# A two-block forward pass on one core: four places where the order of work is changed

## The reference

```
h = x * (1 + sc1) + sh1                          # six modulation rows from w_ada
z, xbc, dt, q, k, v, f = split(h @ w_in)
xs, B, C = split(silu(conv4(xbc)))               # Mamba-2 scan, 16 heads of 64, 4 chunks of 128
y_ssm = rms_norm((scan(xs, dt, A, B, C) + d_skip * xs) * silu(z))
y_att = rms_norm(forgetting_attention(q, k, v, log_sigmoid(f)))     # 16 heads, causal
x = layer_norm(ALPHA * x + (1 + g1) * (concat(y_ssm, y_att) @ w_out))
h = x * (1 + sc2) + sh2
x = layer_norm(ALPHA * x + (1 + g2) * (relu(h @ w_ff_in)**2 @ w_ff_out))
# second block
q, k, v, gb, gc, hin, u = split(rms_norm(x) @ w_in_2)
mix = concat(band_attention(norm(q), norm(k), v), gated_conv(gb, gc, hin), pooling(u))
x = x + mix @ w_out_2
x = x + relu(rms_norm(x) @ w_mlp1_2)**2 @ w_mlp2_2
```

## Time and profile before

| what | value |
|---|---|
| median of 3 runs | 1455.87 us (1450.27 to 1456.78) |
| the profiled execution | 1452.82 us |
| its span, first to last instruction | 1451.1 us |
| mean granted TensorE clock | 0.995 |
| busy share PE, DVE, ACT, POOL | 96%, 47%, 38%, 45% |

### The profile page before, as it was taken

How to read it: one execution, slowest core, us unless ns; L and a number is a source line. 1 busy time by engine, 2 the same in 40 slices (tenths; PEclk the granted TensorE clock), 3 DMA queues, 4 the chain that set the end, 5 groups by cost and what they waited for, 6 DMA issues and landing times.

```text
span 1451.1 us, 17537 instructions
## 1 busy us (share of the span) xinstructions
PE 1398.9 (96%) x6751; PEld 1163.2 (80%) x6751; DVE 679.5 (47%) x991; ACT 546.0 (38%) x792; POOL 659.1 (45%) x523
## 2 busy tenths in 40 slices
PE   2999999999999989999999998999999999999999
PEld 2887787888888878888888876877888888888887
DVE  6677968766622882141325456346514214132131
ACT  0635453576554163141332325324425214133231
POOL 0543855332233855445445544841144544544442
PEclk9999999999999999999999999999999999999999
DMA  9353346633214333232232232320022232223222
GB/s 332 109 146 89 88 146 185 194 118 115 88 31 145 120 90 112 92 107 91 87 116 87 87 116 77 99 87 30 30 88 87 87 103 100 87 88 114 87 92 82
DMA packets 126552, 153.29 MB, mean 106 GB/s; under 512 B 5564, under 2 KB 89808, under 8 KB 126496
## 3 DMA queue, kind: packets, MB, share of 16 engines
q1 hardware_dynamic: 123760, 146.95, 31.9%
q0 software_dynamic: 2192, 5.49, 1.1%
q10 hardware_dynamic: 544, 0.10, 0.0%
HBM read 150.32 MB, written 2.21 MB: 105 GB/s over the span
## 4 chain that ended last, share of the span: by engine, by line
PE 87%; DVE 6%; POOL 3%; ACT 2%; issue 1%; DMA 1%; SPq 0%; DVEq 0%; POOLq 0%; ACTq 0%
PE bank L1558 25%; PE bank L1560 25%; PE bank L1559 25%; PE bank L1703 3%; POOL w_lo L520 2%; PE bank L1693 2%; DVE tmp L1126 1%; PE bank L2050 1%; DMA arena<-in_w_ada_dram 1%; PE bank L1678 1%; PE bank L1874 1%; PE bank L1818 1%; PE bank L1875 1%; ACT w_hi L675 1%; PE bank L1668 1%
## 5 line engine op out<-in xcount | busy, mean ns | idle before, releaser
L520 POOL TENSOR_TENSOR w_lo<-raw,w_hi 128x512 fp32r<-128x512 f32 x428 | 585.6, 1399 | 679.6 <-ACT w_hi L675 678.5
L1558 PE MATMUL bank<-w_hi,a_hi 128*128 128x512 f32 x928 | 365.4, 394 | 13.0 <-DVE a_lo L1037 6.0
L1560 PE MATMUL bank<-w_hi,a_lo 128*128 128x512 f32 x928 | 362.6, 391 | 0.0
L1559 PE MATMUL bank<-w_lo,a_hi 128*128 128x512 f32 x928 | 362.4, 390 | 0.0
L675 ACT ACTIVATE w_hi<-raw 128x2048 fp32r<-128x2048 f32 x107 | 204.8, 1914 | 349.6 <-PE bank L1560 346.6
L1558 PE MATMUL bank<-a_hi,w_hi 128*128 128x512 f32 x800 | 315.6, 394 | 3.4 <-DVE a_lo L1037 2.5
L1560 PE MATMUL bank<-a_hi,w_lo 128*128 128x512 f32 x800 | 312.1, 390 | 0.0
L1559 PE MATMUL bank<-a_lo,w_hi 128*128 128x512 f32 x800 | 312.0, 390 | 0.0
L1558 PEld LDWEIGHTS bank<-w_hi,a_hi 128*128 128x128 f32 x928 | 175.1, 189 | 51.6 <-POOL w_lo L520 6.5
L1560 PEld LDWEIGHTS bank<-w_hi,a_lo 128*128 128x128 f32 x928 | 174.9, 189 | 37.1
L1559 PEld LDWEIGHTS bank<-w_lo,a_hi 128*128 128x128 f32 x928 | 175.2, 189 | 35.5
(11 more groups left out here) (231 smaller groups left out, 1190.1 us busy)
## 6 DMA issues: line engine op xcount, KB each, us to landing
raw<-in_w_mlp_dram SPq DMA_DIRECT2D x32, 1024.0 KB, 5.1
raw<-in_w_in_dram SPq DMA_DIRECT2D x24, 1024.0 KB, 5.2
arena<-in_w_ada_dram SPq DMA_DIRECT2D x18, 1024.0 KB, 5.4
raw<-in_w_ff_in_dram SPq DMA_DIRECT2D x16, 1024.0 KB, 5.3
raw<-in_w_ff_out_dram SPq DMA_DIRECT2D x16, 1024.0 KB, 5.0
raw<-in_w_out_dram SPq DMA_DIRECT2D x12, 1024.0 KB, 5.1
raw<-in_w_in_dram SPq DMA_DIRECT2D x16, 512.0 KB, 5.2
arena<-in_w_ada_dram SPq DMA_DIRECT2D x3, 2048.0 KB, 17.9
```

Source lines behind the costliest of these rows:

```text
L520: last = pool.tensor_tensor(w_lo[:, u0 % 2, cols], raw[:, u0 % 2, cols], w_hi[:, u0 % 2, cols].bitcast(F32), ALU.subtract)
L1558: pe.matmul(out_, hi_a, hi_b, start=start, stop=False)
L1559: pe.matmul(out_, hi_a, lo_b, start=False, stop=False)
L1560: return pe.matmul(out_, lo_a, hi_b, start=False, stop=stop)
```

## The change

The four places are changed like this.

1. `turn_xs(6)` and `turn_xs(7)` come ahead of `z_half(0, 0)` on TensorE. ScalarE's list is as it was.
2. TensorE does `v_half(2, 0)`, `v_half(3, 0)`, `v_half(2, 1)`, `v_half(3, 1)` in place of (2, 0), (2, 1), (3, 0), (3, 1). The tiles lie in banks 0 to 3 in place of 4, 5, 0, 1. ScalarE rounds unit U_QK1 at once after unit U_V + 3, and reads the tiles out later, around the first head's exponentials.
3. ScalarE reads two wo1 tiles ahead of the rounding of U_WO1 + 3. TensorE's second gate row (`g_row(40, ...)`) goes to banks 6 and 7 and ahead of `wo1_half(3, 0)`, and its copies ahead of the first four turned tiles.
4. The first unit of the second block's projection is done for token tiles 0 and 1 over all four k, and then for tiles 2 and 3. It starts when two low parts are made, not four.

```diff
--- before.py
+++ after.py
@@ -108,7 +108,7 @@
             ((6, 2, 8), (7, 0, 1)), ((7, 1, 8),), (), ())
 MIX_K = (6, 7, 4, 5)
 REL_BANKS = ((5, 6), (1, 2))
-V_BANKS = ((4, 5), (0, 1))
+V_BANKS = ((0, 1), (2, 3))
 N3_BANKS = (4, 5, 6, 7, 4, 5, 6, 7)
 
 WO1_HALF = {14: (0, 0), 15: (0, 1), 16: (1, 0), 17: (1, 1)}
@@ -887,14 +887,13 @@
             hi(U_V + 2)
             read_rows(U_V, 0, lambda t: vtok[:, t, 0:512])
             hi(U_V + 3)
+            hi(U_QK1)
 
             def read_v(d):
 
-                act.wait_ge(ticks, 2 * U_V + 2 * d + 2)
+                act.wait_ge(ticks, 2 * (U_V + 3) + d - 1)
                 for n in range(2):
                     act.activation(vtok[:, 2 * (d - 2) + n, 512:1024], bank[V_BANKS[d - 2][n]][:], ACT.Copy).then_inc(evac[1], 1)
-
-            read_v(2)
 
             def wo1_tile(n):
                 act.wait_ge(ticks, 2 * U_WO1 + 2 * (n // 2) + 2)
@@ -912,35 +911,35 @@
                 return bank[b][:, o:o + (q + 1) * P]
 
             for s in range(18):
-                if s == 2:
-                    read_v(3)
+                if s == 1:
+                    read_v(2)
                 elif 3 <= s < 15:
                     split_hi(s + 1, (s - 1) % 2)
                 elif s == 16:
                     wo1_tile(0)
                     wo1_tile(1)
-                if s == 1:
-                    hi(U_QK1, late=1)
-                elif s == 14:
+                if s == 14:
                     hi(U_WO1 + 1)
                 if s >= 2:
                     copy_probT(s - 2, probT)
                 if 1 <= s < 17:
                     probabilities(s - 1, score, prob)
+                if s == 1:
+                    read_v(3)
                 if s % 2 == 0 and 2 <= s < 14:
                     hi(U_QK1 + s // 2)
                 elif s == 17:
                     hi(U_WO1 + 2, late=1)
-            hi(U_WO1 + 3)
             wo1_tile(2)
             wo1_tile(3)
+            hi(U_WO1 + 3)
             wo1_tile(4)
             wo1_tile(5)
             g_row(0, 4, 0)
+            act.wait_ge(ext_out, 32)
+            g_row(1, 6, 3)
             for k in range(4):
                 turned_hi(R_ATT, 1, k, ATT_BANKS[k], v1[:, V_ATT + k:V_ATT + k + 1])
-            act.wait_ge(ext_out, 32)
-            g_row(1, 4, 3)
             act.wait_ge(ticks, 2 * U_WO1 + 7)
             hi(U_WO2)
             act.wait_ge(ticks, 2 * U_WO1 + 8)
@@ -1597,12 +1596,14 @@
                 for j in range(0 if t0 is None else 2, 4):
                     column_tile(u0 + j // 2, j % 2, act_buf, bank[4 * s + j][:], None, i, per)
 
-            def row_half(u0, b, s, act_buf, kk0, first, final, wait=None, i=0, per=0):
+            def row_half(u0, b, s, act_buf, kk0, first, final, wait=None, i=0, per=0, halves=False):
 
 
                 slot = (u0 + b) % 2
                 pe.wait_ge(w_lo_made, at(i, per, u0 + b + 1))
                 order = [(k, t) for k in range(4) for t in range(TB)] if b == 0 else [(k, t) for t in range(TB) for k in range(4)]
+                if halves:
+                    order = [(k, t) for pair in range(2) for k in range(4) for t in (2 * pair, 2 * pair + 1)]
                 for m, (k, t) in enumerate(order):
                     kk = kk0 + k
                     if wait and t == 0:
@@ -1616,13 +1617,13 @@
                     elif b == 1 and m % 8 == 3:
                         last.then_inc(even_done, 1)
 
-            def row_pair(u0, s, n_use, act_buf, t0=None, i=0, per=0, uses=0, tstep=0):
+            def row_pair(u0, s, n_use, act_buf, t0=None, i=0, per=0, uses=0, tstep=0, halves=False):
 
                 if n_use:
                     pe.wait_ge(evac[s], at(i, 4 * uses, 4 * n_use))
                 for b in range(2):
                     wait = None if t0 is None else lambda kk: at(i, tstep, t0 + kk + 1)
-                    row_half(u0, b, s, act_buf, 4 * b, b == 0, b == 1, wait, i, per)
+                    row_half(u0, b, s, act_buf, 4 * b, b == 0, b == 1, wait, i, per, halves and b == 0)
 
             def turn_blocks(turn, n0):
 
@@ -1837,9 +1838,11 @@
             turn_xs(4)
             turn_xs(5)
             pe.wait_ge(cb_evac, 2)
+            turn_xs(6)
+            turn_xs(7)
             z_half(0, 0)
-            for m in range(6, 10):
-                turn_xs(m)
+            turn_xs(8)
+            turn_xs(9)
             z_half(0, 1)
             pe.wait_ge(xs_made, 10)
             ssd_chunk(0)
@@ -1890,20 +1893,23 @@
             late_columns(0)
             row_half(U_V, 1, 0, 0, 4, False, True)
             late_columns(1)
+            pe.wait_ge(evac[0], 4 * N_V[0] + 2)
             v_half(2, 0)
             late_columns(2)
-            v_half(2, 1)
+            pe.wait_ge(evac[0], 4 * (N_V[0] + 1))
+            v_half(3, 0)
             late_columns(3)
-            pe.wait_ge(evac[0], 4 * (N_V[0] + 1))
 
             for s in range(18):
+                if s == 2:
+                    pe.wait_ge(evac[1], 4 * N_V[1] + 4)
                 if s >= 2:
                     probs_t(s - 2, prob)
                 if s < 2:
-                    v_half(3, s)
+                    v_half(2 + s, 1)
                 elif s < 14:
                     if s < 4:
-                        pe.wait_ge(evac[1], 4 * N_V[1] + s + 1)
+                        pe.wait_ge(evac[1], 4 * N_V[1] + s - 1)
                     else:
                         pe.wait_ge(qk_lo, 2 * s + 2)
                     column_tile(U_QK1 + s // 2 - 1, s % 2, 0, bank[s % 2][:])
@@ -1911,7 +1917,6 @@
                     wo1_half(*WO1_HALF[s])
                 if s == 0:
                     pe.wait_ge(ones_set, 4)
-                    pe.wait_ge(evac[1], 4 * N_V[1] + 2)
                 if s >= 2:
                     h = s - 2
                     values(h, probT, lambda k: vtok[:, k, h * HD:h * HD + HD])
@@ -1927,14 +1932,13 @@
             pe.wait_ge(late_made, 1)
             g_row(16, 4)
             wo1_half(2, 1)
+            pe.wait_ge(pt_made, 48)
+            g_row(40, 6)
             wo1_half(3, 0)
-            pe.wait_ge(pt_made, 48)
+            pe.wait_ge(g_made, 4)
             pe.wait_ge(o_made, 16)
             turn(att, 4, 0, ATT_BANKS)
-            pe.wait_ge(g_made, 2)
-            g_row(40, 4)
             wo1_half(3, 1)
-            pe.wait_ge(g_made, 4)
             pe.wait_ge(a_lo_made, T_ATT + 4)
             turn(att, 4, 4, ATT_BANKS)
             pe.wait_ge(yacc_read, 8)
@@ -1954,8 +1958,8 @@
 
             feed_forward(U_FF1, T_X1, T_HID1, N_FF1)
             turn_blocks(1, N_QKV2)
-            pe.wait_ge(a_lo_made, T_N2 + 4)
-            row_pair(U_QKV2, 0, N_QKV2[0], 0, T_N2)
+            pe.wait_ge(a_lo_made, T_N2 + 2)
+            row_pair(U_QKV2, 0, N_QKV2[0], 0, T_N2, halves=True)
             row_pair(U_QKV2 + 2, 1, N_QKV2[1], 0)
             row_pair(U_QKV2 + 4, 0, N_QKV2[0] + 1, 0)
```

## The result

The changed kernel took 1457.76 us (median of 10 executions, 1453.7 to 1460.46). The kernel before, beside it, took 1450.7 us (10 executions, 1450.27 to 1458.2). The ratio is 1.0032, with a 95% interval of 1.0016 to 1.0047. By the ratio, which goes over all executions, that is 4.6 us slower, within 0.5%, as forecast (sum +4.2 us, time 1458.5). Of all executions in this document two took 2875.7 and 7073.6 us, and they stand in no ratio. The profiled execution took 1458.13 us, its span was 1456.4 us and its mean granted clock 0.993.

A forecast was written before the change was run, and what follows sets the result against it. TensorE, busy for 96% of the span, was taken as the bound. Terms +1.5 + 1.7 - 1.8 + 1.7 - 1.5 + 0.9 + 1.7 = +4.2 us gave 1457.0 or 1460.1; forecast 1458.5, range 1451.5 to 1464.

The forecast's parts named there:

- Place 1 (+3.2): Transpositions ahead of the gate: TensorE waits for the twelfth activation, +1.5 us, with a clock fall of +1.7 us.
- Rival 4: All four places work as their order suggests, the first costing nothing: -8.3 us, 1444.5 to 1447.6 us; chance 0.04.
- Place 2 (-0.1): Value tiles by first halves: old wait and fall go, new 2.4 us wait for exponentials, net -1.8, fall +1.7 us.
- I take the fall, +1.7 us: Value tiles: the new 2.4 us wait, close to 2.52 us that cost a fall, is followed by one of 1.7 us.
- the -4.2: Value tiles, best bound: -4.2 us if DVE were free, from the value weight's wait (2.52 us) and its fall (1.7).
- Place 3 (-1.5): Last projection: earlier readings and gate row bring the output weight's products from 465.24 to 464.1; -1.5 us, bounds -0.8 and -1.7.
- Place 4 (+2.6): Second block's query rows: 2.6 us won first, then lost to longer DVE passes; fourth unit 0.9 us later, fall +1.7 us.
- can't start before 889.27: Second block's query rows: DVE's eight activation passes must wait until 889.27 us, when a row lands by DMA.
- Rival 1: DVE's passes aren't lengthened and the query rows win 1.4 us: total +0.2, 1453.0 to 1456.1 us; chance 0.17.
- Rival 2: The clock hardly falls, or falls at other moments: sum -0.9 without three falls, 1451.9 to 1455.0 us; chance 0.17.
- Rival 3: Query rows cascade: fourth weight's low part takes 8 us, TensorE stands 7; total +7.8, 1460.6 to 1463.7 us; chance 0.12.

The follow-up runs named there:

- place 4 alone: The kernel before with only the second block's query rows done by token pairs, starting when two low parts are made; ratio 0.9997 (0.9978 to 1.0015).
- place 3 and place 4 alone: Two runs of the kernel before: only the last projection reordered, ratio 1.0005; only the second block's query rows by token pairs, ratio 0.9997.

## Why the prediction was right, point by point

**Place 1 (+3.2): right.** The wait was 3.85 us (4.0 forecast), the cost +3.0 in the changed kernel and +3.2 alone. Rival 4, by which it costs nothing, is dead. By the traces the +3.0 is 1.9 us more of waiting (3.85 in place of 1.65 and 0.34) and 1.2 us of slower work at the low clock. The run with the steps between the tiles shows the rule: a wait of 1.07 us, within the old slack, cost nothing.

**Place 2 (-0.1): the mechanism right, a term mis-sized.** The wait for the value weight went, and the next thing late was the first maximum, behind the sixth late sum, with 2.84 us of waiting against 2.4. The sum beside POOL took 0.9 us longer, where 0.8 was estimated. The mis-sized step is "I take the fall, +1.7 us": a fall was priced at one size, from one example, and this one came to 3.4 us. The old trace already had one of that size at place 4, nearly half of which met the wait; with 880:884 this row makes 3.4 us:

```profile
876.00:880.00 4.00, 0.00 (x0) 0.66 0.00 0
```

Why the fall at place 2 was the long one stays open. The place came to +2.1. With the late sum out of the way its piece wins the -4.2 that stood in the prediction as a bound.

**Place 3 (-1.5): right in its piece**, -1.6 in the trace; at the end of the execution that much isn't seen (-0.3 among the lowest). The waits of the earlier trace rows for ScalarE are gone, and the products of the output weight wait 1.08 us for DVE in their place (469.75). They still come 1.1 us earlier than before, as forecast, 0.55 of it already ahead of the first tile pair.

**Place 4 (+2.6): the mechanism right, the size off by half.** Four passes met POOL, as forecast, and the fourth weight's low part is the new wait. The wait was 2.24 us and not 3.5: "can't start before 889.27" took the landing of the gain rows as fixed. They were issued at 883.64 and the passes began at 892.16, 8.5 us later; before it was 879.66 to 889.27, 9.6 us. That gave back 1.1 us (why the load landed sooner isn't shown; in the order before, the passes began 20.15 to 20.3 us after the transpositions in six profiles, in the new one 18.9 to 19.2 in three). So the unit starts 0.4 us sooner than before, relative to the transpositions (918.45 - 872.97 = 45.5 us, against 914.9 - 869.0 = 45.9), and with the fall of 1.7 the place costs +1.3. Rival 1's number (-1.4) came true for place 4 alone, but by another cause: a longer fall held TensorE back, and POOL too, which met one pass less. That the meeting is what lengthens the passes is shown by the runs with early gain rows, in both orders; with it gone the changed kernel's piece is 4.1 us shorter.

The Trainium skill (SBUF — State Buffer, Who interferes with whom) says that a VectorE instruction with two SBUF inputs and a GpSimd instruction that reads SBUF contend for a shared pair of ports, which is locked and not split. By that rule the passes need only not overlap with POOL, and the trace agrees. In the changed kernel the engines take turns: POOL's subtractions end at 898.19, 900.43, 902.66 and 904.90, and each of the four passes 1.1 us behind one of them. So a pass takes 2.2 to 2.3 us there and 1.23 us where POOL isn't at work.

**The baseline.** The prediction started from one profile of 1452.8 us and three times whose median was 1455.9, and took a value between. Measured again beside the changed kernel, before's median was 1450.7. Of 33 executions of the kernel before in the last comparison, 21 took 1450.2 to 1451.6 us, one 1453.1 and eleven 1455.8 to 1458.4. Traces of other kernels suggest what parts them; of before itself there is one trace. The run of the old order with early gain rows (1456.4 us) has two falls that come by chance, at 192 us (3.4 us, behind the same wait of 1.19 us that has none in before's profile) and at 252 (1.7 us), together 5.1. So has the run with the steps between the tiles (1456.35 us). Two of the first run's stretches:

```profile
192.00:196.00 4.00, 4.00 (x15) 0.50 0.79 262
252.00:256.00 4.00, 3.31 (x8) 0.57 0.55 148
```

Before's profile (1452.8 us) had the second alone, and the runs of place 3 and place 4 alone (1450.9 and 1449.5 us) had neither. If the groups are these falls, the fall of 1.7 us at place 2 that I counted as removed is missing in most executions of before, and the low end is the one to compare with. Among the lowest five executions of each kernel the median is 1453.7 for place 1, 1454.5 for place 2, 1450.5 for place 3 and 1449.6 for place 4; the 22 lowest of 35 executions of before beside them have 1450.8. This is a rough comparison, since the groups aren't as clear in every kernel. Rival 2 had this half right: falls do come at other moments. But a longer one also made place 2 worse, and the sum did not come out small.

That the total came out near is in part luck, for errors offset each other. In the sum, place 2 was 2.2 us worse than its term, place 4 1.3 us better. In the time, the start was taken some 3.6 us too high (1454.3, where before's median was 1450.7), and the change cost 7.1 us by the medians where +4.2 was forecast. Rival 3 (a cascade at place 4) did not come: its low part took 5.37 us and not 8.

## What to carry to other kernels

Where one engine is busy for 96%, a new order wins in full only if the thing that is late next has been moved too: in the traces the piece of place 2 won 4.2 us after a sum on DVE had been moved, where the order alone cost 2.1. In the changed kernel place 4 won 2.8 us after a small load had been moved, where without that it cost 1.3; by itself it won 1.5 even so. A wait costs what it exceeds the slack at the next waits, plus the slower work if the clock falls behind it. Take several profiles, or the groups of the times, before a fall of the clock in one profile is put into a sum.

## What the runs showed of the hardware that was not expected

- Inside the kernel a fall of the clock to 0.5 came to 1.7 or 3.4 us, and near 2.4 us of waiting it was open whether one came: waits of 2.30, 2.31 and 2.43 us had none, waits of 2.30, 2.36, 2.50 and 2.52 had one. All three profiles with the fall at 192 us that still had this wait show one behind it. The length of the wait alone doesn't decide: with the wait of 2.24 us ahead of the first MLP a fall came in all thirteen profiles.
- Behind a wait of 1.19 us, at 187 to 192 us, the clock fell in five profiles of thirteen, each time for 3.4 us. Two of these five have before's code up to there, and so have six of the eight without the fall. What decides it stays open.
- A longer fall can shorten a later wait: place 4 alone had 3.4 us of low clock at 880 us and no wait for the fourth weight, the changed kernel 1.7 us and a wait of 2.24 us with a second fall. The low clock slowed TensorE, and by it what POOL waits for, so POOL met one DVE pass less.
- When a DVE pass (two SBUF inputs, 128x1024) and POOL's subtractions overlap, both are longer: 2.2 to 2.3 us a pass in place of 1.23, and 8.0 to 8.4 us for the four subtractions in place of 5.05. The pass that was already running when POOL started (892.35 in the run of place 4 with early rows) kept its 1.23 us.
